# Two slot changes in a two-layer block kernel: layer norm in halves, transposes one slot later

## The reference, cut to what matters

```
def conv_branch(u_glu, w_dw, b_dw, g_ln, b_ln, w_out):
    a, gt = jnp.split(u_glu, 2, axis=-1)
    u = a * jax.nn.sigmoid(gt)
    u = lax.conv_general_dilated(u, w_dw[:, None, :], ...) + b_dw     # 31 taps, 1024 channels
    u = jax.nn.silu(layer_norm(u, g_ln, b_ln))
    return u @ w_out
...
y_conv = conv_branch(...)
y_attn = sparse_attn_branch(...)
mixed = (g_conv * y_conv + g_attn * y_attn) @ w_o[l]
x = x + gt1 * rms_norm(mixed, g_post_mix[l])
```

## Time and profile before

| what | value |
|---|---|
| median of 3 runs | 2677.7 us (2673.7 to 2678.93) |
| profiled execution, own time | 2676.21 us |
| its span | 2674.4 us |
| PE busy | 2570.1 us, 96% of the span |
| DVE busy | 1682.0 us, 63% |
| ACT busy | 1282.8 us, 48% |
| granted PE clock, mean over the span | 0.992 |
| HBM rate over the span | 216 GB/s |

### The profile page before, as it was taken

The page is one execution under the profiler, slowest core; times in us unless marked ns, Lnnn a source line. Parts: engine busy times, 40 slices in busy tenths (PEclk is TensorE's granted clock), DMA queues, the critical chain, the costliest instruction groups (busy, mean ns, idle before and its releaser), DMA issues.

```text
span 2674.4 us, 28939 instructions
## 1 busy us (share of the span) xinstructions
PE 2570.1 (96%) x11646; PEld 2103.5 (79%) x11646; DVE 1682.0 (63%) x1914; ACT 1282.8 (48%) x1782; POOL 3.9 (0%) x11
## 2 busy tenths in 40 slices
PE   4999999999989999999999899999999999999998
PEld 4877777877868888888888787778788888888886
DVE  6899899988865555555555545666555454445455
ACT  4535767754454444444444544544454444444443
POOL 0000000000000000000000000000000000000000
PEclk9999999999999999999999999999999999999999
DMA  9998556877946556666555454345455555555553
GB/s 357 336 338 313 174 199 212 292 274 263 385 168 220 205 220 236 236 223 222 204 200 189 162 186 156 142 162 193 165 181 192 186 208 189 193 189 189 189 189 126
DMA packets 80566, 579.17 MB, mean 217 GB/s; under 512 B 8989, under 2 KB 8997, under 8 KB 10544
## 3 DMA queue, kind: packets, MB, share of 16 engines
q1 hardware_dynamic: 78480, 564.82, 58.2%
q10 hardware_dynamic: 1440, 9.81, 0.9%
q0 software_dynamic: 512, 2.69, 0.3%
HBM read 575.17 MB, written 3.68 MB: 216 GB/s over the span
## 4 chain that ended last, share of the span: by engine, by line
PE 86%; DVE 7%; ACT 3%; issue 1%; DMA 0%; ACTq 0%; SPq 0%
PE bank L643 82%; DVE wlo L1453 2%; ACT whi L962 1%; PE bank L607 1%; DVE raw L1463 1%; DVE X L1448 1%; DMA raw<-in_w_in 0%; PE bank L749 0%; ACT SS L1143 0%; PE bank L797 0%; DVE PART L1520 0%; ACT SS L1329 0%; PE bank L732 0%; PE bank L882 0%; DVE SC L1602 0%
## 5 line engine op out<-in xcount | busy, mean ns | idle before, releaser
L1453 DVE TENSOR_TENSOR wlo<-raw,whi 128x1024 fp32r<-128x1024 f32 x882 | 1076.7, 1223 | 936.3 <-ACT whi L962 932.9
L962 ACT ACTIVATE whi<-raw 128x1024 fp32r<-128x1024 f32 x882 | 932.6, 1059 | 1277.9 <-PE bank L643 1181.2
L643 PE MATMUL bank<-whi,HTh 128*128 128x512 f32 x2560 | 704.2, 397 | 7.2 <-ACT HTh L962 5.1
L643 PE MATMUL bank<-wlo,HTh 128*128 128x512 f32 x2560 | 687.7, 390 | 4.2 <-DVE wlo L1453 4.2
L643 PE MATMUL bank<-whi,HTl 128*128 128x512 f32 x2560 | 688.7, 391 | 0.9 <-DVE HTl L1769 0.9
L643 PEld LDWEIGHTS bank<-wlo,HTh 128*128 128x128 f32 x2560 | 481.7, 188 | 107.3 <-DVE wlo L1453 5.4
L643 PEld LDWEIGHTS bank<-whi,HTl 128*128 128x128 f32 x2560 | 482.7, 189 | 104.4 <-DVE HTl L1769 1.4
L643 PEld LDWEIGHTS bank<-whi,HTh 128*128 128x128 f32 x2560 | 472.0, 189 | 107.4 <-issue 16.1
L1463 DVE CUSTOM_DVE_ANT_0 raw<-raw,GT,VECS 128x2048 f32<-128x2048 f32 x96 | 224.7, 2345 | 0.2 <-DMA raw<-in_w_ada 0.2
L643 PE MATMUL bank<-whi,ACTh 128*128 128x512 f32 x704 | 191.5, 394 | 0.0
L643 PE MATMUL bank<-wlo,ACTh 128*128 128x512 f32 x704 | 190.0, 392 | 0.0
(11 more groups left out here) (218 smaller groups left out, 1210.7 us busy)
## 6 DMA issues: line engine op xcount, KB each, us to landing
raw<-in_w_in SPq DMA_DIRECT2D x128, 1024.0 KB, 4.9
raw<-in_w_ada SPq DMA_DIRECT2D x96, 1024.0 KB, 5.6
raw<-in_w_gate SPq DMA_DIRECT2D x88, 1024.0 KB, 4.8
raw<-in_w_up SPq DMA_DIRECT2D x88, 1024.0 KB, 4.8
raw<-in_w_down SPq DMA_DIRECT2D x88, 1024.0 KB, 4.8
raw<-in_w_o SPq DMA_DIRECT2D x16, 1024.0 KB, 6.7
raw<-in_w_out SPq DMA_DIRECT2D x16, 1024.0 KB, 4.8
raw<-in_w_attn_out SPq DMA_DIRECT2D x8, 1024.0 KB, 4.8
```

Of the source, the lines that this page charges most:

```text
L643: i = e.matmul(bank[2 * ch.st + t][:, :], (xl if ps == 1 else xh)[:, k, tk(t)], (lo if ps == 2 else hi)[:, j * 512:j * 512 + 512], start=c ...
L962: return e.activation(dst, src, ACT.Copy, scale=scale)
L1453: e.tensor_tensor(lo, src, r32(hi), S_).then_inc(lo_done, 1)
```

## The change

The sum of squares on PE moves from slot 167 to 168. On DVE `centre` and `norm` are each done in two halves of four blocks: mu and centre 0 in slot 162, centre 1 in 163, mean 167, inv 168, norm 0 in 169, norm 1 in 170, lo from 171 to 174. On ACT sq stands in slot 165, the root in 169, silu and hi in 172 to 175; block c waits for norm half c // 4 alone. All `mix_t` jobs, on all three engines, start one slot later.

```
     cv_dve = steps("cv_dve", [...
-                              "mu", "centre", "mean", "inv", "norm", *[("lo", c) for c in R(8)]])
+                              "mu", ("centre", 0), ("centre", 1), "mean", "inv", ("norm", 0), ("norm", 1),
+                              *[("lo", c) for c in R(8)]])
...  tensor: conv_sums
             i.then_inc(*cv_pe.one("sum"))
-            yield 4
+            yield 5
             w.wait_ge(*cv_act("sq"))
...  tensor, scalar and vector: the start of the mix jobs
-                lane.begin(M["conv"] + 4 * j + 5 + t, mix_t(j, t))
+                lane.begin(M["conv"] + 4 * j + 6 + t, mix_t(j, t))
...  scalar: conv_act
-            w.wait_ge(*cv_dve("centre"))
+            w.wait_ge(*cv_dve("centre", 1))
             e.activation(sq[:, :, :]..., cv[:, :, :]..., ACT.Square).then_inc(*cv_act.one("sq"))
-            yield 2
+            yield 4
             w.wait_ge(*cv_dve("mean"))
             e.activation(stg[5][:, 0:T], stg[5][:, 0:T], ACT.Sqrt).then_inc(*cv_act.one("root"))
-            yield 1
-            w.wait_ge(*cv_dve("norm"))
+            yield 3
             for t in R(2):
                 w.wait_ge(*att_pe[t]("L", 3))
             for c in R(8):
+                w.wait_ge(*cv_dve("norm", c // 4))
                 e.activation(cv[:, c, :], cv[:, c, :], ACT.Silu, ...)
...
-        lane.begin(SUM0 + 1, conv_act())
+        lane.begin(SUM0 + 2, conv_act())
...  vector: conv
-            mean = stg[5][:, 0:T].unsqueeze(1).to_broadcast([128, 8, T])
+            mean = stg[5][:, 0:T].unsqueeze(1).to_broadcast([128, 4, T])
+            halves = [cv[:, 4 * hf:4 * hf + 4, :] for hf in R(2)]
...
-            e.tensor_tensor(cv[:, :, :], cv[:, :, :], mean, S_).then_inc(*cv_dve.one("centre"))
-            yield 3
+            for hf in R(2):
+                e.tensor_tensor(halves[hf], halves[hf], mean, S_).then_inc(*cv_dve.one("centre", hf))
+                yield 1 + 3 * hf
             w.wait_ge(*cv_pe("sqsum"))
-            w.wait_ge(*cv_dve("centre"))
+            w.wait_ge(*cv_dve("centre", 1))
             e.tensor_scalar(stg[5][:, 0:T], bank[7][:, 0:T], 1.0 / 1024, EPS, M_, A_).then_inc(*cv_dve.one("mean"))
             yield 1
             w.wait_ge(*cv_act("root"))
             e.reciprocal(stg[5][:, 0:T], stg[5][:, 0:T]).then_inc(*cv_dve.one("inv"))
+            yield 1
             w.wait_ge(*cv_dve("inv"))
-            e.tensor_tensor(cv[:, :, :], cv[:, :, :], mean, M_).then_inc(*cv_dve.one("norm"))
-            yield 1
+            for hf in R(2):
+                e.tensor_tensor(halves[hf], halves[hf], mean, M_).then_inc(*cv_dve.one("norm", hf))
+                yield 1
             for c in R(8):
                 w.wait_ge(*cv_act("hi", c))
                 e.tensor_tensor(CTl[:, c, :], cv[:, c, :], r32(CTh[:, c, :]), S_).then_inc(*cv_dve.one("lo", c))
```

More of the change, by code:

```diff
@@ L1020, in evict @@
                         w.wait_ge(*gt_pe(0, 3))
-                        w.wait_ge(*cv_dve("norm"))
+                        w.wait_ge(*cv_dve("norm", 1))
                         for u in R(2):
```

## The result

The changed kernel takes 2670.87 us (median of 17 runs, 2669.46 to 2674.37), the kernel before 2676.99 (17 runs). The ratio is 0.9979, with a 95% interval of 0.9972 to 0.9987: 6.1 us less (3.5 to 7.5 by the interval), just over 0.2%. The forecast was 2671.8 us, with a chance of 0.46 that the gain would be over 0.2%.

The account below looks back on a forecast made before the run. The prediction took PE's weight matmuls as the bound, the kernel being as fast as PE is fed. 2676.2 - 5.0 - 1.2 + 0.3 = 2670.3 us on the profiled execution, so 2671.8 as median; range 2667.0 to 2677.0.

Parts of the forecast that it names:

- Part A: Mixed branches' transposes: one slot later, PE's four waits for X (4.3 us) and small losses go, 5.0 us gained.
- Part B: Layer norm during attention's matmuls: new order and halves cut PE's losses from 6.3 to 5.1 us, 1.2 gained.
- the walk: Layer norm: the prediction's step-by-step timing of the DVE and ACT queues, putting conv's start at 603.2 us.
- Rival 1: Layer norm: the halves work whole, PE's waits before conv vanish, 6.3 us gained, 2666.7 us; chance 0.12.
- rival 2: Layer norm gives nothing: PE's clock drops after the 2.3 us wait, late loads add more; 2672.5 to 2674; chance 0.20.
- Part C: Stretch behind, wo: late weight transfers take back 0 to 1.8 us of PE's gain; 0.3 us taken.
- Rival 3: Transfers in wo take it back: stretch 680 to 735 keeps its pace, only 1 us stays, 2676.7; chance 0.08.
- Rival 4: Slower: `hi 0` comes late through slow transfers and starves PE of low parts; 2678.3, up to 2684; chance 0.10.

Follow-up runs that it names:

- e5: The changed kernel with the reload of x started in slot 220 instead of 198; 2671.08 us, ratio 0.9976.
- e6: The changed kernel with the edits of e3 and e5 together; 2666.63 us, ratio 0.9961.
- e7: e6 with norm half 1 one slot later still on DVE (slot 172) and lo from slot 173; 2668.6 us, ratio 0.9962.
- e1: The kernel before with only the mixed branches' transposes one slot later; 2672.95 us against 2678.24, ratio 0.9980.
- e2: The changed kernel with the transposes' later slot undone, so only the layer norm's new slots and halves; 2676.3 us, ratio 0.9995.
- e8: The changed kernel run once more, unaltered, for a second profiled execution; 2670.75 us, ratio 0.9977.
- e3: The changed kernel with DVE's reciprocal and what follows it (norm halves, lo) one slot later; 2667.37 us, ratio 0.9964.
- e4: The changed kernel with centre and norm each as one instruction over all eight blocks; 2672.76 us, ratio 0.9979.

## Why the prediction was right, step by step

**Part A (5.0 us).** Right in mechanism and size. All four waits for X went. Conv's stretch gained 3.3 (53.46 to 50.13). What wo gains of the fourth wait is read where nothing holds PE up: piece 204 starts 30.05 us after wo's first matmul before, and 28.18 in e5, e6 and e7, so 1.9. That makes 5.2. e1 shows the part by itself: 4.7 in stretches, that is 5.2 less 0.5 that wo loses again; its 5.3 in time agrees within its interval.

**Part B (1.2 us).** Right in mechanism. With 2.87 us added for the later start, the walk stands beside the trace: sum of squares 570.07 (570.06), reciprocal 579.4 after a wait of 4.1 (579.30, 4.02), the load issued at 582.4 (582.20), the split of 174 at 587.3 (586.98), `hi 0` done at 590.7 (590.4), PE's third pass of 174 at 595.5 (595.27), conv's start at 606.1 (606.12). PE's waits were foreseen as 0.5, 0.6, 2.3 and 1.0 and came as 0.20, 0.45, 2.06 and, in e2 and e8, 0.7. Rival 1 (the whole 6.3) fell: the 4.02 us before the reciprocal and the 2.06 of PE are its refutation, and e3 shows that the order of the two queues is the cause, since one slot took them away and gave 3.5 to 3.8 us.

The size came out closer than the parts that it is made of. Counted as the prediction counts, e8 loses 4.9 us between the sum of squares and conv (32.5 us for ten pieces), against 5.1 forecast. But 3.5 of it are waits, where the prediction had 4.55, and 1.4 come along with the waits, where it had 0.55: two errors that cancel, which is luck. PE waits about as long as before (3.5 against 3.6); what e2 and e8 gain is that the clock did not fall (1.7 before), less 0.4 of small losses. In the changed kernel's first profile it is the other way round: the waits fell to 2.7 and the clock fell too.

**The clock (rival 2).** It fell after 2.06 us of idle time in the changed kernel and after 2.10 in e5, and not after 2.10 in e2 and e8. Where it fell the stretch was 56.00 and 56.05, else 55.77 and 55.73: 0.3 us, where the prediction's rival had 0.6 and a bare count of the slow matmuls (1.35, 1.91 and 1.76 in place of 1.08 each) gives 1.8. The wait for the low part of 176 is missing in the executions in which the clock fell, so DVE's delay and PE's slowness overlap. The rival's mechanism happened and its result did not, since its other half, slower transfers (0.5 to 1.5 us more than 4.85), did not come: both took 4.8 (582.20 to 586.98, 590.21 to 595.00).

**Part C (0.3 us).** The term that was mis-sized, and in the wrong place. Without a loss wo's stretch would have fallen by 1.9, to 99.8. It fell by 0.2 in the changed kernel, 1.1 in e8 and 1.4 in e1, so the loss was 1.7, 0.8 and 0.5 (1.2 in e3, 1.9 in e4, just outside the bound of 1.8). The prediction charged it to the split for piece 208 and had the load of piece 204 (676.92) "again released in step". It was released nearly in step: its issue came 3.2 us earlier and PE's need of it 3.5. But the larger delay of this profile, 1.3 us, was at piece 204 all the same, because the transfer took 10.9 us and not 9.3. These rows are the issue, the split and the start of piece 204 in the changed kernel, then that start in the kernel before:

```profile
673.71 0.33 SPq L582 DMA_DIRECT2D raw<-in_w_o  x1
684.61 1.06 ACT L963 ACTIVATE whi<-raw 128x1024 fp32r<-128x1024 f32 x1 [5.28 <-PE bank L644]
685.72 1.20 PE L644 MATMUL bank<-whi,HTh 128*128 128x512 f32 x4 [1.13 <-ACT whi L963]
```
```profile
687.92 1.07 PE L643 MATMUL bank<-whi,HTh 128*128 128x512 f32 x4
```

(The profile puts the split's wait down to PE, but the piece that this split needs ended more than 5 us earlier, so it waited for the transfer.) At piece 208, the prediction's place, a wait of PE is listed in e8 alone, 0.16 us. e5, e6 and e7, with the reload of x out of the way, start piece 204 without a delay, which ties the loss to the reload. What sets the transfer's length from run to run stays open. Rival 3, by which only 1 us of the whole gain stays, did not hold: at least 4.7 stay. But it names what eats a part: in the changed kernel's first profile wo nearly kept its old pace (101.46 against 101.66), with a new wait of 1.1 us, under the 2 that the rival asks.

**The sum.** 5.0 + 1.2 - 0.3 = 5.9 us was forecast. In stretches the first profile shows 5.2 + 1.2 - 1.7 = 4.7 and e8 5.2 + 1.4 - 0.8 = 5.9 (rounded); the medians show 6.1, with 3.5 to 7.5 by the interval. So the sum is right, and its closeness to a few tenths is more than the runs can confirm. Rival 4 (slower) had no counterpart: the two transfers that it needs late came in time.

## What to carry to other kernels

When a chain that runs over two in-order engines is laid out in slots, write down for each link which slot its producer has on the other engine: a consumer one slot before its producer delays all that is queued behind it, here weight parts that had nothing to do with the chain. A wait in such a queue also holds the release of buffers, so it comes back a few slots later as a late transfer; look for the second wait there. Splitting an instruction paid nothing where the next engine was waiting for something else (e4): test the halves apart from the slots.

## What was not expected of the hardware

Idle times of nearly the same length, 2.06 and 2.10 us, were followed by a fall of PE's clock to 1.2 GHz in two profiled executions (the changed kernel and e5), and 2.10 us was not in two others (e2 and e8), whose order of work up to there is the same; the earlier trace rows has 3.05 without a fall. So the length of the idle time alone does not decide it, and what does is not shown. The row of e5, which has 1.81 where e8 has 1.19:

```profile
594.32 1.81 PE L644 MATMUL bank<-wlo,ATh 128*128 128x512 f32 x4 [2.10 <-DVE wlo L1454]
```

The fall's cost can be hidden, too: 1.8 us of slow matmuls moved the stretch by 0.3, because the engine that PE would have waited for next used the time.
